# Linear attention in pieces between the units of the input projection, with the score differences on VectorE

## The reference

```
n = modulate(rms_norm(h)); parts = n @ w_in         # q k v | gq gk gv gz low | gates
la = log_sigmoid(low @ w_dec + b_dec) / 16          # per direction, 4 heads x 64
def step(s, (qi, ki, vi, gi)):                      # chunk after chunk
    b = cumsum(gi)
    o = (qi * exp(b)) @ s + (sum_d qi kj exp(b_i - b_j), j <= i) @ vi
    s = exp(b_last) * s + (ki * exp(b_last - b)).T @ vi
o = o_forward + flip(o_backward)
gla = rms_norm(o, g_gla) * silu(gz)
h += gate * ((sigmoid(g0) * (attn @ w_b0) + sigmoid(g1) * (gla @ w_b1)) @ w_out)
```

## Time and profile before

| | us |
|---|---|
| median of 3 runs (3025.79 to 3031.61) | 3028.68 |
| profiled execution, its own time | 3022.72 |
| its span, first to last instruction | 3020.9 |
| last matmul of the input projection starts | 1424.02 |
| first square of `qk_act` starts | 1701.31 |
| TensorE busy | 2803.9 |
| VectorE busy | 1502.4 |
| ScalarE busy | 556.7 |
| GpSimd busy | 508.0 |

### The profile page before, as it was taken

The page is one execution under the profiler, slowest core; times in us unless marked ns, Lnnn a source line. Parts: engine busy times, 40 slices in busy tenths (PEclk is TensorE's granted clock), DMA queues, the critical chain, the costliest instruction groups (busy, mean ns, idle before and its releaser), DMA issues. The chain is left out here.

```text
span 3020.9 us, 35198 instructions
## 1 busy us (share of the span) xinstructions
PE 2803.9 (93%) x14298; PEld 2292.2 (76%) x14298; DVE 1502.4 (50%) x2336; ACT 556.7 (18%) x1039; POOL 508.0 (17%) x400
## 2 busy tenths in 40 slices
PE   8999999999999999999456869998999999999998
PEld 3888888888888788887255647776777888888887
DVE  7544445444434611111776488885645444444444
ACT  4100000000000411112422447773011000000002
POOL 0065655554200000000063001211000000000001
PEclk9999999999999999999666679999999999999999
DMA  7112122222111211332000100002421111111111
GB/s 271 46 60 70 60 68 89 84 84 94 54 35 42 84 37 43 94 98 75 0 1 1 42 1 1 1 1 91 156 68 35 49 49 44 49 46 49 49 49 70
DMA packets 192127, 176.65 MB, mean 58 GB/s; under 512 B 6989, under 2 KB 148602, under 8 KB 191994
## 3 DMA queue, kind: packets, MB, share of 16 engines
q1 hardware_dynamic: 186016, 164.22, 17.1%
q10 hardware_dynamic: 5978, 10.56, 0.9%
HBM read 155.89 MB, written 18.87 MB: 58 GB/s over the span
## 5 line engine op out<-in xcount | busy, mean ns | idle before, releaser
L219 PE MATMUL psum<-nh,wh 128*128 128x512 f32 (+2 forms) x1688 | 612.9, 363 | 1.4 <-DVE wl L196 1.4
L220 PE MATMUL psum<-nl,wh 128*128 128x512 f32 (+2 forms) x1688 | 612.2, 363 | 0.0
L221 PE MATMUL psum<-nh,wl 128*128 128x512 f32 (+2 forms) x1688 | 611.8, 362 | 0.0
L194 DVE CAST wh<-raw 128x1024 fp32r<-128x1024 f32 x175 | 125.8, 719 | 695.0 <-PE psum L221 689.4
L219 PEld LDWEIGHTS psum<-nh,wh 128*128 128x128 f32 (+1 forms) x1688 | 316.7, 188 | 53.8 <-DVE wl L196 1.8
L221 PEld LDWEIGHTS psum<-nh,wl 128*128 128x128 f32 (+1 forms) x1688 | 316.5, 188 | 51.4
L220 PEld LDWEIGHTS psum<-nl,wh 128*128 128x128 f32 (+1 forms) x1688 | 316.7, 188 | 50.6
L844 DVE SCALAR_TENSOR_TENSOR h<-psum,gates,h 128x512 f32<-128x512 f32 (+1 forms) x400 | 270.8, 695 | 150.9 <-PE psum L221 149.1
L219 PE MATMUL psum<-hidh,wh 128*128 128x512 f32 (+1 forms) x880 | 329.2, 374 | 11.3 <-DVE hidl L828 7.6
L812 ACT ACTIVATE silu_a<-psum 128x512 f32<-128x512 f32 (+1 forms) x110 | 61.2, 556 | 1488.1 <-PE psum L221 1488.1
L220 PE MATMUL psum<-hidl,wh 128*128 128x512 f32 (+1 forms) x880 | 324.8, 369 | 0.0
(11 more groups left out here) (251 smaller groups left out, 3866.7 us busy)
## 6 DMA issues: line engine op xcount, KB each, us to landing
raw<-in_w_ffn_up_dram SPq DMA_DIRECT2D x88, 512.0 KB, 3.9
mod_part<-in_w_mod_dram SPq DMA_DIRECT2D x96, 256.0 KB, 4.2
...
mod_raw<-in_w_mod_dram SPq DMA_DIRECT2D x12, 1024.0 KB, 13.7
gates_saved<-staged ACTq DMA_DIRECT2D x40, 256.0 KB, 2.0
merge_gate<-gates_saved SPq DMA_DIRECT2D x8, 1024.0 KB, 5.0
...
```

What stands on the lines that cost most here:

```text
L194: nc.vector.tensor_copy(wh[:, par, 0:n], raw[:, par, 0:n]).then_inc(panel_split, 1)
L219: pe.matmul(o, hi_w, hi_x, start=first, stop=False)
L220: pe.matmul(o, hi_w, lo_x, start=False, stop=False)
L221: return pe.matmul(o, lo_w, hi_x, start=False, stop=last)
```

## The change

The panels are reordered: low, gk, k, v, gv, gq, gz, q, gates. k, v, q and the gate panels are copied through `staged` to DRAM (`kvq_dram`, `gate_dram`), and the Sigmoid moves to `merge_act`. After the six paired units only two banks (1 and 2) carry units, so unit u waits until unit u - 2 is copied out. The other six are for the linear attention, whose code is cut into pieces: after each unit every engine calls `decay_*`, `state_*` and `intra_*` with the unit's number, and tables of unit numbers say what is done there. The score work is now by head pair and half: four groups of eight levels are 32 items of eight matmuls, five items in four units, so that every fourth unit from 49 to 73 has two. The units with outputs (`OUT_UNITS`) are 55, 62, 68 and 74. An item's differences are made by VectorE one unit before its products. The finished `gla_f` goes to DRAM and comes back at the end with k, q and v. `glah` is then made by ScalarE in `qk_act` and `glal` by GpSimd, which does nothing else of this part.

```diff
+    win = [(C_LOW, 2 * RANK, ALL, KEPT, lambda t0, w: low_f[0:2 * RANK, t0:t0 + w])]
+    win += [(C_GK + i * P, P, ALL, KEPT, lambda t0, w, i=i: gk_f[:, i, t0:t0 + w]) for i in range(2)]
+    win += [(C_K, P, ALL, COPIED, lambda t0, w: kvq_dram[0, :, t0:t0 + w])]
+    win += [(C_V, P, ALL, COPIED, lambda t0, w: kvq_dram[1, :, t0:t0 + w])]
+    win += [(C_GV + i * P, P, ALL, KEPT, lambda t0, w, i=i: gv_f[:, i, t0:t0 + w]) for i in range(4)]
+    win += [(C_GQ + i * P, P, LAT, KEPT, lambda t0, w, i=i: gq_f[:, i, t0:t0 + w]) for i in range(2)]
+    win += [(C_GZ + i * P, P, LAT, SILU, lambda t0, w, i=i: gate_dram[i, :, t0:t0 + w]) for i in range(4)]
+    win += [(C_Q + i * P, P, LAT, COPIED, lambda t0, w, i=i: kvq_dram[2 + i, :, t0:t0 + w]) for i in range(4)]
+    win += [(C_GATE + i * P, P, LAT, COPIED, lambda t0, w, i=i: gate_dram[4 + i, :, t0:t0 + w]) for i in range(16)]
...
-    WIN_BANKS = (4, 6, 7, 5, 0, 3, 1, 2)
...
+    PAIR_UNITS = 6
+    PAIR_BANKS = (4, 6, 7, 5, 0, 3)
+    RING_BANKS = (1, 2)
...
+                sp.wait_ge(dec_zero, 1)
+                sp.dma_start(wdec[0:RANK, 0:256], w_decay[0, 0]).then_inc(dec_loaded, 16)
+                sp.dma_start(wdec[RANK:2 * RANK, 256:512], w_decay[0, 1]).then_inc(dec_loaded, 16)
+            if i in GZ_PANELS:
+                g = GZ_PANELS.index(i)
+                if g >= 1:
+                    gla_store(sp, g - 1)
+                gz_load(sp, g)
+        gla_store(sp, N_GROUPS - 1)
...
-            if u >= 8:
-                pe.wait_ge(win_evac, u - 7)
+            if u >= PAIR_UNITS + 2:
+                pe.wait_ge(win_evac, u - 1)
             for k in range(KT):
                 mm = unit_k(u, k)
             done(u, mm)
+            decay_pe(pe, u)
+            state_pe(pe, u)
+            intra_pe(pe, u)
...
+                nc.scalar.activation(staged[:, n % 4, 0:w], src, ACT.Silu if kind == SILU else ACT.Copy)\
                     .then_inc(win_evac, 1)
+                act.wait_ge(win_evac, u + 1)
+                act.dma_start(target(t0, w), staged[:, n % 4, 0:w]).then_inc(saved[n % 4], 16)
+            decay_act(act, u)
+            state_act(act, u)
+            intra_act(act, u)
...
-        for i, (_, width, _, _) in enumerate(win):
-            if i >= 2:
-                split_panel(dve, pn(panel0 + i), KT * width)
+        dve.wait_ge(h_saved, 16)
+        nc.vector.memset(wdec[0:2 * RANK, :], 0.0).then_inc(dec_zero, 1)
+        split_panel(dve, pn(panel0 + 2), KT * win[2][1])
+        for u in range(PAIR_UNITS, N_UNITS):
+            i, c = win_units[u]
+            if c == 0 and i + 1 < len(win):
+                split_panel(dve, pn(panel0 + i + 1), KT * win[i + 1][1])
+            decay_dve(dve, u)
+            state_dve(dve, u)
+            intra_dve(dve, u)
...
+    LOGIT_UNITS = [6, 7, 8, 9, 10, 11, 35, 36, 37, 38, 39, 40]
...
+    LN_UNITS, SCAN_UNITS = [8, 11, 37, 40], [10, 13, 39, 42]
+    DEXP_UNITS, KEY_UNITS = [11, 14, 40, 43], [12, 15, 41, 44]
...
+    VTURN_UNITS = [27, 28, 29, 30, 31]
+    BATCH_UNITS = [32, 33, 34, 35, 36, 37, 42, 43, 44, 45, 46, 47]
...
+    N_GROUPS = 4
+    N_ITEMS = N_GROUPS * N_SCORES
...
+    SCORE_BANKS = ((0, 3), (4, 5))
+    OUT_PAIR = (6, 7)
+    GZ_PANELS = (22, 26, 30, 33)
+
+    ITEM_UNITS = [49 + 4 * n // 5 for n in range(N_ITEMS)]
+    OUT_UNITS = [ITEM_UNITS[N_SCORES * g + N_SCORES - 1] + 1 for g in range(N_GROUPS)]
+    TAKE_UNITS = [max(ITEM_UNITS[n], OUT_UNITS[n // N_SCORES - 1] if n % N_SCORES == 0 and n else 0) + 1
+                  for n in range(N_ITEMS)]
+    QDEC_UNITS = [ITEM_UNITS[N_SCORES * g + 4] for g in range(N_GROUPS)]
...
+    def intra_pe(pe, u):
+        if u in OUT_UNITS:
+            g = OUT_UNITS.index(u)
+            t, hf = divmod(g, 2)
+            pe.wait_ge(g_pred, 2 * N_SCORES * (g + 1))
+            pe.wait_ge(g_qd, 2 * (g + 1))
...
+                    ch = 4 * hf + cc
+                    o = ps[OUT_PAIR[par]][:, cc * P:(cc + 1) * P]
+                    pe.matmul(o, vtok(ch, 2 * t + par), scores[:, par, cc, :], start=True, stop=False)
                     for d in range(2):
+                        mm = pe.matmul(o, states[r, d, ch, t, :], qdec[r, d, cc * P:(cc + 1) * P],
                                        start=False, stop=(d == 1))
...
+        if u - 1 in OUT_UNITS:
+            g = OUT_UNITS.index(u - 1)
+            pe.wait_ge(o_sq, 2 * g + 2)
+            pe.wait_ge(g_oc, 2 * g + 2)
+            for par in range(2):
+                pe.matmul(halves_of(OUT_PAIR[par]), ones, squares_of(par), start=True, stop=True).then_inc(o_ss, 1)
...
+            pe.wait_ge(g_qk, 2 * n + 2)
+            if n >= 2:
+                pe.wait_ge(g_pred, 2 * (n - 1))
+            else:
+                pe.wait_ge(g_state, N_STATES)
+            for cc in range(4):
+                for par in range(2):
+                    r = slice(DK * par, DK * par + DK)
+                    here = slice(cc * P, (cc + 1) * P)
+                    w = gk_f[r, t, tok][:, here] if lv == 0 else eks[n % 2][r, here]
+                    mm = pe.matmul(ps[SCORE_BANKS[n % 2][par]][:, here], w, eqs[n % 2][r, here],
+                                   start=True, stop=True)
+            mm.then_inc(g_sc, 1)
...
+            if ITEM_UNITS[n] == u + 1 and n % N_SCORES:
+                act.wait_ge(g_lq, 4 * decayed(n) + 4)
+                for e in (eqs[n % 2], eks[n % 2]):
+                    nc.scalar.activation(e[:, :], e[:, :], ACT.Exp, scale=1.0 / GATE_NORM).then_inc(g_eq, 1)
+
+    def differences(dve, n):
+        _, lv, t, tok = item(n)
+        if n >= 2:
+            dve.wait_ge(g_sc, n - 1)
...
+        nc.vector.tensor_tensor(qr, fr, fref, ALU.subtract).then_inc(g_lq, 1)
+        nc.vector.tensor_tensor(ql, bl, bref, ALU.subtract).then_inc(g_lq, 1)
+        nc.vector.tensor_tensor(kl_, fref, fl, ALU.subtract).then_inc(g_lq, 1)
+        nc.vector.tensor_tensor(kr_, bref, br, ALU.subtract).then_inc(g_lq, 1)
...
+    def intra_dve(dve, u):
+        for n in range(N_ITEMS):
+            if TAKE_UNITS[n] != u:
+                continue
+            g, lv, t, tok = item(n)
+            dve.wait_ge(g_sc, n + 1)
...
+                    nc.vector.copy_predicated(dst, m, src).then_inc(g_pred, 1)
+        if u - 1 in OUT_UNITS:
+            g = OUT_UNITS.index(u - 1)
+            if g >= 1:
+                dve.wait_ge(g_stored, 32 + 16 * g)
+            for par in range(2):
+                dve.wait_ge(o_sq, 2 * g + par + 1)
+                nc.vector.tensor_copy(gla_f[:, par, :], ps[OUT_PAIR[par]][:, :]).then_inc(g_oc, 1)
...
+        if u - 1 in QDEC_UNITS:
+            g = QDEC_UNITS.index(u - 1)
+            t, hf = divmod(g, 2)
+            for d in range(2):
+                dve.wait_ge(g_qde, 2 * g + d + 1)
+                nc.vector.scalar_tensor_tensor(qdec[:, d, :], gq_f[:, t, hf * 512:(hf + 1) * 512], DK ** -0.5,
+                                               qdec[:, d, :], ALU.mult, ALU.mult).then_inc(g_qd, 1)
...
+                dve.wait_ge(g_eq, 2 * decayed(n) + 2)
+                nc.vector.scalar_tensor_tensor(eqs[n % 2][:, :], gq_f[:, t, tok], DK ** -0.5, eqs[n % 2][:, :],
+                                               ALU.mult, ALU.mult).then_inc(g_qk, 1)
+                nc.vector.tensor_tensor(eks[n % 2][:, :], gk_f[:, t, tok], eks[n % 2][:, :], ALU.mult)\
                     .then_inc(g_qk, 1)
+        for n in range(N_ITEMS):
+            if ITEM_UNITS[n] == u + 1 and n % N_SCORES:
+                differences(dve, n)
+        if u - 2 in OUT_UNITS:
+            g = OUT_UNITS.index(u - 2)
+            dve.wait_ge(z_loaded, 16 + 32 * (g + 1))
+            for par in range(2):
+                dve.wait_ge(o_rs, 2 * g + par + 1)
+                dve.wait_ge(g_oc, 2 * g + par + 1)
+                nc.vector.scalar_tensor_tensor(gla_f[:, par, :], gla_f[:, par, :], cols_b[:, B_GGLA:B_GGLA + 1],
+                                               gla_r[par][:, :], ALU.mult, ALU.mult).then_inc(o_norm, 1)
+                dve.wait_ge(o_norm, 2 * g + par + 1)
+                nc.vector.tensor_tensor(gla_f[:, par, :], gla_f[:, par, :], gz_s[par][:, :], ALU.mult)\
+                    .then_inc(o_gate, 1)
...
+    def weave_end_sp(sp):
+        sp.wait_ge(g_oz, N_GROUPS)
+        wait_saved(sp, len(staged_units))
+        sp.dma_start(k_f[:, :], kvq_dram[0]).then_inc(kvq_loaded, 16)
+        sp.dma_start(q_f[:, :, :], kvq_dram[2:6, :, 0:SEQ].rearrange("n p t -> p n t")).then_inc(kvq_loaded, 16)
+        sp.dma_start(v_f[:, :], kvq_dram[1]).then_inc(kvq_loaded, 16)
+        sp.dma_start(rope_t[:, :, :], rope.rearrange("a p t -> p a t")).then_inc(rope_loaded, 16)
+        sp.wait_ge(panel_used, merge_p0)
+        sp.wait_ge(g_stored, 32 + 16 * N_GROUPS)
+        sp.dma_start(gla_n[:, :, :], gla_dram).then_inc(gla_back, 16)
+
+    def gla_low_pool(pool):
+        for hd in range(GLA_HEADS):
+            pool.wait_ge(o_hi, hd + 1)
```

(38 more changed lines are left out.)

607 lines of the change are left out of this document (265 added, 342 removed).

## The result

The changed kernel takes 2886.57 us (median of 4 runs, 2884.4 to 2889.21) against 3028.19 us (4 runs, 3025.79 to 3031.61): ratio 0.9532, 95% interval 0.9515 to 0.9548, 141.6 us gained where 136 were forecast (2893 us, range 2868 to 2925). The profiled execution took 2889.21 us.

What follows compares the result with a forecast made beforehand. The serial linear attention, 276.9 us of short chained steps, was taken as the bound; 103 + 14 + 6 + 14 + 3 + 1 = 141 come back, 136 gained, so 3028.7 - 136 = 2893 us, range 2868 to 2925.

Steps and rivals of the forecast that it cites:

- The bound: Linear attention between projection and first square: 276.9 us that no engine fills, a chain of short steps; this serial stage goes.
- TensorE's own work, 103: Linear-attention pieces placed between units: values, logits, keys and states, scores, outputs and sums add 103 us at full clock.
- Waits in the weave, 14: Units 49 to 74: TensorE waits 14 us for VectorE's queue, mostly in units with two items; upper end 49.
- The clock, 6: Weave: a few dips of TensorE's clock from waits and weak work cost 6 us; ends 0 and some 40.
- The end, 14, and the copies, 3: After the last matmul: 14 us to the first square while k, q, v load; four copies delay the square root 3 us.
- GpSimd at the end, 1: GpSimd's `glal` subtractions beside VectorE's work on v and q: one slowed product each, 1 us, at most 3.
- More waits (2925): Rival: VectorE bounds the weave; each item adds 1 us, 32 us in all, giving 2925 us; chance 0.15.
- Nothing waits (2873): Rival: in the weave no clock dips and no losses in doubled units, 20 us less, 2873 us; chance 0.12.
- The half clock in the score units: Rival: in units 49 to 74 the clock falls and stays down, 212 us more, 3105 us; chance 0.03.
- The end was not longer: Rival: transfers at the end take longer, so 14 us becomes 25, 2904 us; within the main case, no separate chance.
- The changed differences: Differences moved to VectorE: two-SBUF-input VectorE instructions block against GpSimd reading SBUF (product 2.00 against 1.22 us), which favours the move.

Runs made afterwards that it cites:

- the unwoven kernel: Against the changed kernel, the same linear-attention pieces all follow the last unit of the panels, on every engine; 3097.04 us, ratio 1.0226 to before.
- the early loads: Against the changed kernel, loads of k, q and v are issued once their own stores have landed, not behind the last panels' stores; 2874.32 us.
- twice the differences: Against the changed kernel, VectorE makes each item's four differences twice and ScalarE waits for both sets; 2906.62 us.

## Why the prediction was right, and where its terms were off

*The bound.* The serial stage of 276.9 us was for the most part a chain of handovers and not work that TensorE needs; moved between units, little more than TensorE's own part of it comes back. Right, and shown by the unwoven kernel, in which the same instructions cost 210 us more.

*TensorE's own work, 103.* Measured 103.4 from the start of each piece to the next start: logits 10.9 (9 forecast), values 4.0 (5.5), keys and states 13.2 (17), scores 36.6 (33), outputs 31.9 (30), sums 6.8 (8 to 9). Halving the outputs' time at 0.50 was the right step, though short by an eighth:

```profile
1412.67 0.49 PE L1457 MATMUL psum<-scores,vlat 128*128 128x128 f32 x2
1413.09 0.71 PE L1459 MATMUL psum<-qdec,states 64*128 64x128 f32 x4
1413.73 0.49 PE L1457 MATMUL psum<-scores,vlat 128*128 128x128 f32 x2
```

One head and chunk each 1.06 us, where half of the earlier trace rows gave 0.94. The score pieces, 3.6 us over the forecast in all, end in the half of a visit's turnover (see above) that is booked here and not with the panel steps; that this is the excess is argued and not shown.

*Waits in the weave, 14.* Mis-sized; measured 6.7: unit 53 cost 1.38 (2.5 forecast), 57 0.19 (1.1), 58 1.10 (2.0), 65 2.93 (4.0), 69 0.21 (0.7), 71 0.69 (1.6), 73 0.18 (1.1), and 59 nothing (1.0). The count's starting point was right: in units 53, 57, 65, 69 and 73 the differences of the second item begin 0.1 us after TensorE has done the unit before (P). Its sizes were not. TensorE and VectorE in units 64 and 65, where P is 1436.31:

```profile
1436.31 0.50 PE L220 MATMUL psum<-nh,wh 128*128 128x512 f32 x1
...
1444.97 3.28 PE L1482 MATMUL psum<-eq,ek 64*128 64x128 f32 x32 [2.93 <-DVE ek L1590]
```

```profile
1436.42 0.43 DVE L1537 TENSOR_TENSOR eq<-cum 128x256 f32<-128x256 f32 x1
...
1437.77 0.74 DVE L1601 SCALAR_TENSOR_TENSOR gla_f<-gla_f,cols_b,gla_r 128x512 f32<-128x512 f32 x1
...
1440.55 0.69 DVE L195 CAST wh<-raw 128x1024 fp32r<-128x1024 f32 x1
1441.27 1.22 DVE L197 TENSOR_TENSOR wl<-raw,wh 128x1024 fp32r<-128x1024 f32 x1
1442.41 1.32 DVE L1560 COPY_PREDICATED scores<-cst,psum 128x512 f32<-128x512 int32 x2
1443.63 0.67 DVE L1588 SCALAR_TENSOR_TENSOR eq<-gq_f,eq 128x512 f32<-128x512 f32 x1
```

From the differences at 1436.42 to the first product's end the queue never stands still, so here VectorE's queue sets the wait, as said. But the count added up whole durations, while in a queue most instructions start some 0.08 us before the one ahead of it has ended: four differences take 1.35 us (1.5 counted), the split 1.86 (1.95), two takes 1.21 to 1.27 (1.35), two products 1.20 (1.4). In unit 57 the first item's products so end at P + 5.9 instead of 6.2, and TensorE, whose 24 matmuls and the steps at their edges take 5.67 instead of 5.44, waits 0.19 instead of 0.75. The second items' products, for which 0.35 was counted in each such unit, were not waited for.

*The clock, 6.* Mis-sized; I can place 1 us of it, which is in the 103.4. The 32 score matmuls behind the 2.93 us wait took 3.28 instead of 2.36 us, and the windows are at 0.97 once and else 1.00 (0.93 in the same window when the kernel was run again, 1.00 with the early loads, so the dip comes and goes). The rule of the Trainium skill that I weighed ("TensorE: Matmul & The Clock Gate", Part 1) gave 0, and this trace comes near it. The unwoven kernel does not agree with it: one output takes 1575.92 - 1574.04 = 1.88 us in it, the half clock, and TensorE is busy for 15.7 of the 16 us from 1573. Its last outputs began at the full clock behind a wait of 1.43 us, two of them 1.06 us each, and from 1742.8 on ran at 0.51 for 11.2 us in which TensorE never idled. What the rows show is that such work stayed at 2.4 GHz for 8 us when it came behind panels (eight outputs of 1.06 from 1411.7), and that behind a stretch of stalls it ran at 1.2 GHz from its start or fell to it.

*What the sum left out.* The longer panel steps at the edges of the visits, some 0.2 us each time, 10.5 us in all, most of it the seen half of the turnover. It and the smaller waits nearly cancel: forecast 103 + 14 + 6 = 123 from unit 6 to the last matmul, measured 103.4 + 6.7 + 10.5, and 1.6 that I cannot place, 122.2. That the sum came so near is in this part luck: two terms were too large by 12 us together, and one was missing.

*The end, 14, and the copies, 3.* 13.4 and 2.3. The cause is shown by the early loads. *GpSimd at the end, 1:* the four subtractions run from 1584.3 to 1593.6, and VectorE's six instructions on v beside them take 0.41 to 0.69 as they do in before; none of them has two inputs in SBUF. No hit is to be seen. The stretch from the first square on is only 0.5 us longer in all, less than the 2.3 of the copies, so about 2 us were saved there. In before 18.0 us of VectorE's work on norm, gate and split stood behind the first square and are gone; whether they make the 2 us was not traced.

*The rivals.* More waits (2925) would have needed 1 us more for each item on VectorE; twice the differences added 38.4 / 28 = 1.4 us an item and the time was 2906.6, so 32 us for 1 us an item was priced too high. Nothing waits (2873): half true, the clock stayed up but for one dip, and of the 14 us of waits 6.7 came. The half clock in the score units did not come. The end was not longer.

*The changed differences.* I had named contention as speaking for VectorE. The contention is there and does not matter; the measured worth of the move is 0 to -5 us.
